# Both layer norms of a two-block transformer kernel by token halves, with the chunks around them multiplied half by half

## The reference

```
def layer_norm(x, g, b):
    mu = jnp.mean(x, axis=-1, keepdims=True)
    var = jnp.mean(jnp.square(x - mu), axis=-1, keepdims=True)
    return ((x - mu) * lax.rsqrt(var + LN_EPS)).astype(x.dtype) * g + b

for i in range(2):                      # even_mixer, then odd_mixer
    u = x * (1.0 + sc) + sh             # modulation of layer i
    y = mixer(u @ w_in ...) @ w_out     # the "mixer output product"
    x = layer_norm(alpha * x + gt * y, ln_g[i], ln_b[i])
p = rms_norm_2(x, norm_mix) @ w_in_2    # second block: the next product after norm 2
```

## Time and profile before

| | us |
|---|---|
| median of three runs | 2410.95 |
| the profiled execution | 2408.33 |
| its span | 2406.5 |
| TensorE busy | 2351.4 |
| VectorE busy | 1442.4 |
| ScalarE busy | 1094.7 |

### The profile page before, as it was taken

How to read it: one execution, slowest core, us unless ns; L and a number is a source line. 1 busy time by engine, 2 the same in 40 slices (tenths; PEclk the granted TensorE clock), 3 DMA queues, 4 the chain that set the end, 5 groups by cost and what they waited for, 6 DMA issues and landing times.

```text
span 2406.5 us, 30234 instructions
## 1 busy us (share of the span) xinstructions
PE 2351.4 (98%) x12212; PEld 1912.5 (79%) x12212; DVE 1442.4 (60%) x1416; ACT 1094.7 (45%) x1147; POOL 70.6 (3%) x116
## 2 busy tenths in 40 slices
PE   7999999999999999999999989999999999999998
PEld 5667887887678788887878877788888888888886
DVE  3445477755956887567667685665545545445454
ACT  4322554544653534546555352455544334334333
POOL 1000001000000000000000000000000000000000
PEclk9999999999999999999999999999999999999999
DMA  9994578856965697555545311754665565565563
GB/s 370 321 332 154 180 248 281 266 169 248 385 221 187 228 367 237 203 191 157 193 140 177 103 30 42 270 183 149 185 183 184 192 192 175 201 192 182 194 210 123
DMA packets 234022, 496.07 MB, mean 206 GB/s; under 512 B 21568, under 2 KB 23680, under 8 KB 226848
## 3 DMA queue, kind: packets, MB, share of 16 engines
q1 hardware_dynamic: 221360, 438.99, 55.2%
q0 software_dynamic: 11984, 54.13, 6.1%
q10 hardware_dynamic: 544, 1.05, 0.1%
HBM read 487.84 MB, written 6.29 MB: 205 GB/s over the span
## 4 chain that ended last, share of the span: by engine, by line
PE 68%; DVE 5%; ACT 1%; issue 1%; DVEq 0%; ACTq 0%
PE banks L2950 61%; PE banks L3023 2%; PE banks L3391 1%; PE banks L3289 1%; PE banks L3486 1%; DVE decayed_a L2032 0%; DVE inverse_products L2642 0%; PE banks L3380 0%; PE banks L2927 0%; DVE inverse_by_chunk L2643 0%; PE banks L3286 0%; DVE decayed_b L2032 0%; DVE scores_diag L2057 0%; PE banks L3660 0%; DVE decayed_a L2041 0%
## 5 line engine op out<-in xcount | busy, mean ns | idle before, releaser
L1717 DVE TENSOR_TENSOR weights_lo<-weights_raw,weights_hi 128x2048 fp32r<-128x2048 f32 x348 | 795.3, 2286 | 686.2 <-ACT weights_hi L862 676.6
L862 ACT ACTIVATE weights_hi<-weights_raw 128x2048 fp32r<-128x2048 f32 x348 | 665.6, 1913 | 884.2 <-PE banks L2950 811.5
L2950 PE MATMUL banks<-weights_hi,acts_hi 128*128 128x512 f32 (+1 forms) x2032 | 514.2, 395 | 2.6 <-DVE latent_keys L1879 1.4
L2950 PE MATMUL banks<-weights_hi,acts_lo 128*128 128x512 f32 (+1 forms) x2032 | 501.3, 389 | 0.0
L2950 PE MATMUL banks<-weights_lo,acts_hi 128*128 128x512 f32 (+1 forms) x2032 | 500.2, 388 | 0.0
L2950 PEld LDWEIGHTS banks<-weights_hi,acts_hi 128*128 128x128 f32 x2032 | 377.1, 189 | 88.3 <-issue 11.5
L2950 PEld LDWEIGHTS banks<-weights_hi,acts_lo 128*128 128x128 f32 x2032 | 382.0, 188 | 79.0
L2950 PEld LDWEIGHTS banks<-weights_lo,acts_hi 128*128 128x128 f32 x2032 | 380.8, 188 | 78.0
L2950 PE MATMUL banks<-weights_hi,hidden_hi 128*128 128x512 f32 x288 | 71.5, 390 | 0.0
L2950 PE MATMUL banks<-weights_lo,hidden_hi 128*128 128x512 f32 x288 | 71.1, 389 | 0.0
L2950 PE MATMUL banks<-weights_hi,hidden_lo 128*128 128x512 f32 x288 | 71.1, 389 | 0.0
(11 more groups left out here) (614 smaller groups left out, 2270.7 us busy)
## 6 DMA issues: line engine op xcount, KB each, us to landing
weights_raw<-in_w_in_e SPq DMA_DIRECT2D x72, 1024.0 KB, 5.5
weights_raw<-in_w_up SPq DMA_DIRECT2D x64, 1024.0 KB, 5.5
weights_raw<-in_w_down SPq DMA_DIRECT2D x64, 1024.0 KB, 5.1
weights_raw<-in_w_in SPq DMA_DIRECT2D x44, 1024.0 KB, 5.0
modulation_weights<-in_w_ada SPq DMA_DIRECT2D x64, 512.0 KB, 10.8
raw_eight<-in_w_ada SPq DMA_DIRECT2D x32, 1024.0 KB, 8.5
weights_raw<-in_w_in_o SPq DMA_DIRECT2D x32, 1024.0 KB, 5.4
gate_piece<-in_w_ada POOLq DMA_DIRECT2D x32, 512.0 KB, 5.5
```

Source lines behind the costliest of these rows:

```text
L862: eng.activation(WHI[:, c % 2, :, 0:n], RAW[:, sl, :, 0:n], ACT.Copy).then_inc(hi_ready, 1)
L1717: eng.tensor_tensor(WLO[:, c % 2, :, 0:n], RAW[:, c % 4, :, 0:n], WHI[:, c % 2, :, 0:n].bitcast(F32), ALU.subtract).then_inc(lo_ready, 1)
L2950: ins = eng.matmul(BANKS[:, par * 2 + h, 0:s.n], x[:, kt + k, h * P:(h + 1) * P], w[:, c % 2, k, 0:s.n], start=(kc == 0 and k == 0 and m = ...
```

## The change

The last two chunks of the first product are multiplied together, first both for the upper 128 tokens, then both for the lower (`last_by_half`). The first two chunks of the next product are also done half by half (`first_by_half`). The transposed tiles are now 4 feature tiles x 128 tokens, of one half each, in the order of `HALF_TILES` (block, half). The upper half is normalised by ScalarE (`upper_norm`), the lower by VectorE (`lower_norm`), and ScalarE's gain and bias take four activations of 128 columns per tile instead of two of 256.

```
+    NORMED = {"x1T": 1, "x2T": 2}
+    HALF_TILES = [(0, 0), (1, 0), (0, 1), (1, 1), (2, 0), (2, 1), (3, 0), (3, 1)]
...
@@ -936,7 +943,9 @@
             if following:
                 hi(following, following.g0, 0, 0)
             last()
-            if following:
+            if norm:
+                norm(lambda: hi(following, following.g0, 0, 1))
+            elif following:
                 hi(following, following.g0, 0, 1)
...
+        def upper_norm(b):
+            eng.activation(XN[:, b, 0, :], XN[:, b, 0, :], ACT.Identity, scale=STAT[:, 66:67], bias=STAT[:, 67:68])\
+               .then_inc(S("act_rows"), 1)
+
+        def normed_hi(name, *tiles):
+            n = NORMED[name]
+            for pos in tiles:
+                b, h = HALF_TILES[pos]
+                jj, k = J[name] + pos, 16 * (n - 1) + pos
+                eng.wait_ge(S("norm_cols"), n)
+                if k >= 4:
+                    eng.wait_ge(S("tile_lo"), k - 3)
+                bank_full(eng, jj)
+                for i in range(4):
+                    f = 4 * b + i
+                    ins = eng.activation(normed_tile(k)[:, i, :], bank(jj)[:, i * P:(i + 1) * P], ACT.Identity,
+                                         scale=NORMC[:, 0, f:f + 1], bias=NORMC[:, 1, f:f + 1])
+                    if i < 3:
+                        ch.add(ins)
+                free(ins, jj)
+                ch.wait()
+                copied(eng, jj)
+                eng.activation(half_tile(XTH, b, h), normed_tile(k), ACT.Copy).then_inc(S("tile_hi"), 1)
+
+        def residual_norm(name):
+            def steps(second_hi):
+                root(STAT[:, 66:67])
+                roots[0] += 1
+                eng.wait_ge(S("square_in"), roots[0])
+                upper_norm(0)
+                second_hi()
+                upper_norm(1)
+                normed_hi(name, 0)
+                root(STAT[:, 70:71])
+                normed_hi(name, 1)
+                upper_norm(2)
+                upper_norm(3)
+            return steps
+
...
-        stream(st["in_o"], after={1: normed_hi("x1T", 1, 0, 1, 2), 2: normed_hi("x1T", 1, 3), 20: pool_hi(0), 23: pool_hi(1),
+        stream(st["in_o"], after={1: lambda: normed_hi("x1T", 2, 3), 2: lambda: normed_hi("x1T", 4, 5), 3: lambda: normed_hi("x1T", 6, 7), 20: pool_hi(0), 23: pool_hi(1),
...
+        def upper_scale():
+            mean, rstd = STAT[:, 64:65], STAT[:, 66:67]
+            roots[0] += 1
+            eng.wait_ge(S("root_out"), roots[0])
+            ch.link(eng.reciprocal(rstd, rstd))
+            ch.add(eng.tensor_scalar(STAT[:, 67:68], mean, rstd, -1.0, ALU.mult, ALU.mult))
+            ch.done("square_in")
...
                     ch.done("square_in")
+                    if h == 0:
+                        upper_scale()
+                        lo(following, following.g0, 0, 0)
...
-        def norm_blocks(*blocks):
+            stream(s, each, after=after)
+        def lower_norm(*blocks):
+            mean, rstd = STAT[:, 68:69], STAT[:, 70:71]
+                if b == 0:
+                    roots[0] += 1
+                    eng.wait_ge(S("root_out"), roots[0])
+                    ch.link(eng.reciprocal(rstd, rstd))
+                ch.add(eng.tensor_scalar(XN[:, b, 1, :], XN[:, b, 1, :], mean, rstd, ALU.subtract, ALU.mult))
                 ch.done("block_normed")
...
+        def normed_acts(name, s):
+            normed_lo(name, 0)
+            lower_norm(0)
             lo(s, s.g0, 0, 1)
-            normed_lo(name, n, 2, 3, 4, 5)
+            normed_lo(name, 1)
+            lower_norm(1, 2, 3)
+            normed_lo(name, 2, 3)
...
+        in_after = {1: lambda: normed_acts("x1T", st["in_o"]), 2: lambda: normed_lo("x1T", 4, 5),
+                    3: lambda: (normed_lo("x1T", 6, 7), gain(0, 32)), 4: lambda: gain(1, 32), 5: lambda: bias(0), 6: lambda: bias(1)}
...
+        def last_by_half(s):
+            b, c0 = s.nblk - 1, s.nblk * s.kc - 2
+            par, (xh, xl) = (s.b0 + b) % 2, s.x or (XTH, XTL)
+            for h in range(2):
+                for c in (c0, c0 + 1):
+                    kt = s.kt0(b) + 4 * ((c % s.kc + s.rot) % 4)
+                    if h == 0:
+                        acts_ready(s, kt)
+                        eng.wait_ge(hi_ready, s.g0 + c + 1)
+                    for m, (x, w) in enumerate(((xh, WHI), (xl, WHI), (xh, WLO))):
+                        if h == 0 and m == 1:
+                            eng.wait_ge(lo_ready, s.g0 + c + 1)
+                        for k in range(4):
+                            ins = eng.matmul(BANKS[:, par * 2 + h, :], x[:, kt + k, h * P:(h + 1) * P], w[:, c % 2, k, :],
+                                             start=False, stop=(c > c0 and k == 3 and m == 2))
+                        if h == 1 and m == 1:
+                            ins.then_inc(hi_used, 1)
+                    if h == 1:
+                        ins.then_inc(chunk_used, 1)
+                    elif c > c0:
+                        ins.then_inc(S("upper_full"), 1)
...
+        def first_by_half(s):
+            name, par = s.acts, acc_pair(s, 0)
+
+            def part(c, h):
+                pos = HALF_TILES.index((c, h))
+                eng.wait_ge(S("tile_hi"), CUT[name] + pos + 1)
+                if h == 0:
+                    eng.wait_ge(hi_ready, s.g0 + c + 1)
+                for m, (x, w) in enumerate(((XTH, WHI), (XTL, WHI), (XTH, WLO))):
+                    if m == 1:
+                        eng.wait_ge(S("tile_lo"), TILES_BEFORE[name] + pos + 1)
+                        if h == 0:
+                            eng.wait_ge(lo_ready, s.g0 + c + 1)
+                    for k in range(4):
+                        ins = eng.matmul(BANKS[:, par * 2 + h, :], x[:, 4 * c + k, h * P:(h + 1) * P], w[:, c % 2, k, :],
+                                         start=(c == 0 and k == 0 and m == 0), stop=False)
+                    if h == 1 and m == 1:
+                        ins.then_inc(hi_used, 1)
+                if h == 1:
+                    ins.then_inc(chunk_used, 1)
+
+            normed_tiles(name, 0, 1)
+            eng.wait_ge(block_out, 2 * s.b0 + 2)
+            part(0, 0)
+            normed_tiles(name, 2)
+            part(1, 0)
+            normed_tiles(name, 3, 4, 5)
+            part(0, 1)
+            part(1, 1)
+            normed_tiles(name, 6, 7)
...
```

More of the change, by code:

```diff
@@ L881, in _, with stream @@
         held = []
-        def stream(s, each=None, after=None, hold=False, following=None):
+        def stream(s, each=None, after=None, hold=False, following=None, norm=None):
             after = after or {}
@@ L1312, in wait_jobs @@
                 jobs_out(eng, n)
[L1315 to L1337, removed]
         def pool_hi(b):
@@ new lines, in lower_norm, with normed_lo @@
+                ch.add(eng.tensor_scalar(XN[:, b, 1, :], XN[:, b, 1, :], mean, rstd, ALU.subtract, ALU.mult))
+                ch.done("block_normed")
+        def normed_lo(name, *tiles):
+            for pos in tiles:
+                b, h = HALF_TILES[pos]
+                eng.wait_ge(S("tile_hi"), CUT[name] + pos + 1)
+                eng.tensor_tensor(half_tile(XTL, b, h), normed_tile(16 * (NORMED[name] - 1) + pos),
+                                  half_tile(XTH, b, h).bitcast(F32), ALU.subtract).then_inc(S("tile_lo"), 1)
@@ new lines, in normed_tiles @@
+        def normed_tiles(name, *tiles):
+            n = NORMED[name]
+            for pos in tiles:
+                b, h = HALF_TILES[pos]
+                eng.wait_ge(*((S("block_normed"), 4 * (n - 1) + b + 1) if h else (S("act_rows"), 2 + 4 * (n - 1) + b + 1)))
+                jj = J[name] + pos
+                bank_free(eng, jj)
+                for i in range(4):
+                    ins = eng.transpose(bank(jj)[:, i * P:(i + 1) * P], XN[:, b, h, i * P:(i + 1) * P], ident)
+                full(ins, jj)
@@ L2941, in chunk @@
                 for k in range(4):
+                    tile = 2 * (kt // 4) + 2 if s.acts in NORMED else (kt + k) // 2 + 1
                     if first_tiles is not None and k % 2 == 0 and m == 0:
-                        eng.wait_ge(S("tile_hi"), CUT[s.acts] + (kt + k) // 2 + 1)
+                        eng.wait_ge(S("tile_hi"), CUT[s.acts] + tile)
                     if first_tiles is not None and k % 2 == 0 and m == 1:
-                        eng.wait_ge(S("tile_lo"), first_tiles + (kt + k) // 2 + 1)
+                        eng.wait_ge(S("tile_lo"), first_tiles + tile)
                     if s.acts == "cross_o" and k == 2 and m == 0:
@@ L2977, in stream @@
             peeled = s.nblk if not s.loop else 2 * (max(after) // 8 + 1) if after else 0
+            halves = s.by_half and not s.loop and s.direct
+            if s.acts in NORMED:
+                first_by_half(s)
             for c, (b, kc) in enumerate(s.order[0:peeled * s.kc]):
+                if s.acts in NORMED and c < 2:
+                    continue
+                if halves and c == s.nblk * s.kc - 2:
```

(8 more changed lines are left out.)

43 lines of the change are left out of this document (11 added, 32 removed).

## The result

The changed kernel takes 2418.35 us (median of nine, 2415.11 to 2422.07) against 2410.89 (nine, 2406.55 to 2413.96). The ratio is 1.0031, interval 1.0023 to 1.0040: 7.5 us slower (5.5 to 9.6). The forecast was 2417 and slower. The profiled execution took 2418.5, its span 2416.7.

What follows compares the result with a forecast made beforehand. TensorE, busy 98% of the span, bounds the kernel. Losses 0.41 + 1.98 + 2 x 1.85 = 6.1 us on the profiled 2408.33 make 2414.4; the median stands 2.6 above, so 2417.0, range 2409 to 2423.

Steps and rivals of the forecast that it cites:

- ScalarE's order and the table load: ScalarE's queue delays chunk 3 by 0.41 us in the first place, 1.98 in the second, where the square-root table loads.
- the walk: Engine queues followed in both places from the first product's last matmul issued (zero); chunk 3 at 27.29 and 28.68 before clock.
- the 12.6 us that could be won at most: Both 4.5 us wait places: some 6.3 us lost in each, 0.5% together, the most the change could win.
- rival 2: Not slower: ScalarE's tile at 1.65, clock stays full; 2.0 and 0.4 us won in the places, 2408.5; chance 0.08.
- rival 3: Much slower: tiles at 2.56, clock loss 3.0 net per place; 12.7 us lost, 2423.6; chance 0.14.
- The clock: TensorE at half clock for 4.55 us from chunk 0's first upper part on; 1.85 us lost per place.
- Rival 1: Clock stays full in both places because bursts cut the idle time; 2.4 us lost, 2413.4, no change; chance 0.24.

Runs made afterwards that it cites:

- e1_fill: Changed kernel plus throwaway identity transposes in TensorE's new waits in both places; 2414.45 us, ratio 1.0013 to the kernel before.
- e5_before_fill: Kernel before the change plus 42 throwaway identity transposes in each of the two 4.5 us waits; 2411.53 us, ratio 1.0002.
- e4_all: Changed kernel plus throwaway transposes ahead of chunk 0's upper part, old tiles for chunks 2 and 3, early table load; 2407.36 us, ratio 0.9981.
- e2_pair: Changed kernel with the tiles of chunks 2 and 3 back to 2 feature tiles x 256 tokens; 2412.45 us, ratio 1.0002 to the kernel before.
- e3_root: Changed kernel plus one throwaway square root in the second place, loading the table early; 2417.28 us, ratio 1.0025 to the kernel before.
- e10_before_again: Kernel before the change, nothing edited, executed once more for a second profile; 2410.23 us.
- e11_few: Like e4_all, but 7 long products of identity times 512 constant columns per place instead of short throwaway transposes; 2413.46 us, ratio 1.0012.
- e8_all_again: The kernel of e4_all, executed once more for a second profile; 2407.99 us.

## Why the prediction was right

Point by point, first place, forecast and measured, after zero:

| step | forecast | measured |
|---|---|---|
| upper block 0 on ScalarE | -0.8 | -0.78 |
| tile 0 ready, upper part starts | 4.82 | 4.75 |
| lower part of chunk 0, with 1.85 for the clock | 14.70 | 14.75 |
| copy for chunk 2, with the same | 16.77 | 16.93 |
| activation of 128 columns, tile | 0.46, 2.13 | 0.45, 2.11 |
| chunk 3, with the same | 29.14 | 30.41 |
| second place, upper part | 6.21 | 6.18 |
| second place, chunk 3 | 30.53 | 29.83 |

**ScalarE's order and the table load**: forecast 0.41 + 1.98 = 2.4 us. With the clock held (e1_fill) the same order costs 0.04 + 1.64 = 1.7 us against the first profile of before: right in place and sign, 0.7 too large. Most of this is the transposes: the walk priced them by a row's duration (1.04 for eight, 1.6 for twelve), but from start to start twelve take 1.23 in e1_fill (794.55 to 795.78), 0.4 less in each place. For the same reason the 12.6 us that could be won at most are some 2 us too low. How large the term is depends on what it is laid against, since the kernel before has the half clock in its places too: against its second profile it is 0.63 + 2.03 = 2.7, against the kernel before with the clock held (e5_before_fill) 1.08 + 2.48 = 3.6. The price between the 256- and the 128-column rows carried the term: rival 2 needed tiles under 1.9 and is out with 2.11, and so are rival 3's 2.56. By the Trainium skill ("ScalarE: Activation LUTs", What ACT_TABLE_LOAD costs) my estimate of the tile was 2.28; the measured 2.11 decides.

**The clock**: forecast 1.85 a place, 3.7. Against e1_fill it was 3.49 + 1.49 = 5.0. This is the term that was mis-sized most, 1.3 too small, and in opposite ways in the two places. In the first the upper part lost 2.40 us (5.25 against 2.85), where 2.28 were forecast; but the wait ahead of chunk 2, which my walk contained, let the clock fall a second time, and I had not drawn that from my own wait. It is more than the 3.0 that rival 3 had as the highest. In the second place the fall came 2.8 us before the upper part (1096.8 and 1099.65), in the first 0.9 us before it (789.6 and 790.55), so less of it met work; chunk 2's wait of 1.88 us brought no second fall there. Where the fall comes was not in the walk, and it differs between executions (the second profiles above). Rival 1 (the clock stays) is out; e1_fill shows what its time would have been, 2414.4, where 2413.4 was forecast.

In e1_fill the waits held nothing but transposes, and the clock stayed at 1. The Trainium skill ("TensorE: Matmul & The Clock Gate", Part 4) says of the transpose mode that the full clock "doesn't engage" for it and that it "doesn't count as PE-busy the same way"; whether these transposes run in that mode no run shows, and for them the measurement decides.

**The sum**: 6.1 forecast, 1.7 + 5.0 = 6.7 in the places, 7.5 (5.5 to 9.6) in the medians: part of the closeness is luck, as one term was too large and the other too small. Against the second profile of before the places lose 4.12 + 3.52 = 7.6. The 1.5 us of the late stretch stood in no forecast; how much of them the timed runs carry is open. That these two are the causes is shown by taking them away: with the clock held, the old tiles for chunks 2 and 3 and the table early (e4_all), the same split is 4.6 us (2.2 to 7.0) faster than the kernel before.

## What to carry to other kernels

Splitting a wait into bursts does not make it cheaper if the clock falls in the bursts' gaps: ask which instructions will run at half clock afterwards, and price them. When a tile is cut along the columns of one engine's instruction, count what the engine behind it pays per instruction; cut only the tiles that are needed early. Throwaway work that holds the clock gave 3.9 us in the changed kernel, but nothing that the medians show in the kernel before, so try it beside the other edits and not by itself; its size must be read from the very instruction used.

## What the runs showed of the hardware

- Throwaway transposes in waits of 1.4 to 4.5 us kept the clock at 1 through both places (e1_fill, e4_all, e5_before_fill); without throwaway work it fell in both places of every profile (before twice, the changed kernel, e2_pair, e3_root).
- After a wait of 1.9 us ahead of chunk 2 the clock fell, 0.7 to 1.1 us after work had resumed, in three of four places (the changed kernel and e3_root); in the fourth, 1.88 us, it stayed. In the kernel before, TensorE stood for 3.2 us from 665.6 on and the clock stayed at 1, so the length of a wait alone did not decide it.
- In the kernel before, the clock stood at one half for 6.8 us in each place of one profile and for 3.4 us in the next (e10_before_again).
- A product of a float32 128x128 by 512 columns shows as two records of 0.43 us (e11_few).
- A stretch far behind the change, part of it at half clock, took 15.79 us in the kernel before and 20.31 with all three edits (16.24 and 20.22 in the second profiles). The profiled executions of e4_all and e8_all_again lie 3.8 and 0.6 us over that kernel's median, so how much of it the timed runs carry is open.
